# One attention's exponentials on ScalarE: the output copy between the two heads, and a wait for each head

## What is computed

```
def swa_mixer(h, w_in, q_g, k_g, sinks, memq_g, w_out, mem_k, mem_v):
    ...
    sc = jnp.where(mask[None, :, None, None], sc + bias[None, None], NEG_INF)
    ...
    p = jax.nn.softmax(jnp.concatenate([sc, sink], axis=-1), axis=-1)[..., :-1]
    o = jnp.einsum('bnhgqc,bnchd->bnqhgd', p.astype(vv.dtype), vv).reshape(b, s, SWA_Q_WIDTH)
    m = memory_attention(q_mem, memq_g, mem_k, mem_v)
    return jnp.concatenate([o, m], axis=-1) @ w_out
```

## Time and profile before

| | us |
|---|---|
| median of 3 runs | 2240.65 |
| the 3 runs | 2238.53, 2240.79, 2240.65 |
| profiled execution | 2238.2 |
| its span | 2236.4 |
| TensorE busy | 2188.2 (98%) |
| VectorE busy | 1716.2 (77%) |
| ScalarE busy | 1404.4 (63%) |
| GpSimd busy | 139.1 (6%) |

### The profile page before, as it was taken

One profiled execution on the slowest core, in us unless ns is written; L12 is line 12 of the kernel. 1 busy time (PEld: TensorE's weight loads), 2 busy tenths in 40 slices (PEclk: granted clock), 3 DMA queues, 4 the chain that ended last, 5 costly groups with the idle time before them and its releaser, 6 DMA issues.

```text
span 2236.4 us, 36111 instructions
## 1 busy us (share of the span) xinstructions
PE 2188.2 (98%) x11690; PEld 1871.0 (84%) x11690; DVE 1716.2 (77%) x2248; ACT 1404.4 (63%) x1865; POOL 139.1 (6%) x142
## 2 busy tenths in 40 slices
PE   8999998899999999999999999999999999999998
PEld 7889987778888888888888888788889888888987
DVE  7956656589999999999999999966576556657654
ACT  4264444568788888878787878744655444465543
POOL 8400005020000000000000000000010000001000
PEclk9999999999999999999999999999999999999999
DMA  6235554169999999999999999954355655435564
GB/s 223 84 121 192 183 184 151 41 219 374 350 363 378 356 350 357 374 356 361 353 374 367 367 352 359 346 170 151 122 175 190 189 185 188 149 129 168 184 197 142
DMA packets 151054, 552.00 MB, mean 247 GB/s; under 512 B 16736, under 2 KB 16864, under 8 KB 150752
## 3 DMA queue, kind: packets, MB, share of 16 engines
q1 hardware_dynamic: 150448, 548.77, 68.9%
q10 hardware_dynamic: 432, 1.02, 0.1%
HBM read 548.67 MB, written 1.05 MB: 246 GB/s over the span
## 4 chain that ended last, share of the span: by engine, by line
PE 87%; issue 7%; ACT 3%; DVE 3%; DMA 0%; POOL 0%; DVEq 0%; ACTq 0%; POOLq 0%
PE L L1997 58%; PE L L2050 10%; PE L L2509 5%; PE L L2605 3%; PE TB L2065 2%; PE L L2014 2%; PE SC L2228 2%; PE L L2168 1%; ACT SMX L759 1%; PE SC L2391 1%; PE SC L2399 1%; DVE wlo L1146 1%; PE L L2278 1%; PE SC L2135 1%; PE TB L2154 0%
## 5 line engine op out<-in xcount | busy, mean ns | idle before, releaser
L1146 DVE TENSOR_TENSOR wlo<-deep,whi 128x1024 fp32r<-128x1024 f32 x682 | 810.0, 1223 | 43.4 <-ACT whi L663 12.7
L663 ACT ACTIVATE whi<-deep 128x1024 fp32r<-128x1024 f32 x682 | 713.1, 1060 | 133.0 <-PE L L1997 130.4
L1146 DVE TENSOR_TENSOR wlo<-raw,whi 128x1024 fp32r<-128x1024 f32 x353 | 428.1, 1227 | 256.1 <-ACT whi L663 251.7
L663 ACT ACTIVATE whi<-raw 128x1024 fp32r<-128x1024 f32 x353 | 367.8, 1058 | 314.0 <-PE L L1997 151.2
L1997 PE MATMUL L<-whi,xhi 128*128 128x512 f32 (+1 forms) x1136 | 447.5, 394 | 2.8 <-DVE wlo L1146 2.4
L1997 PE MATMUL L<-whi,xlo 128*128 128x512 f32 (+1 forms) x1136 | 441.6, 389 | 0.0
L1997 PE MATMUL L<-wlo,xhi 128*128 128x512 f32 (+1 forms) x1136 | 441.3, 388 | 0.0
L1997 PEld LDWEIGHTS L<-whi,xhi 128*128 128x128 f32 x1136 | 213.7, 188 | 48.5 <-DVE wlo L1146 6.2
L1997 PEld LDWEIGHTS L<-whi,xlo 128*128 128x128 f32 x1136 | 213.6, 188 | 45.1
L1997 PEld LDWEIGHTS L<-wlo,xhi 128*128 128x128 f32 x1136 | 213.8, 188 | 42.1
L1997 PE MATMUL L<-whi,mhi 128*128 128x512 f32 x448 | 175.3, 391 | 0.0
(11 more groups left out here) (378 smaller groups left out, 3468.8 us busy)
## 6 DMA issues: line engine op xcount, KB each, us to landing
deep<-wm SPq DMA_DIRECT2D x679, 512.0 KB, 5.5
raw<-wm SPq DMA_DIRECT2D x245, 512.0 KB, 3.8
raw<-w SPq DMA_DIRECT2D x112, 512.0 KB, 4.3
mbuf<-mem SPq DMA_DIRECT2D x2, 1024.0 KB, 8.6
const<-const SPq DMA_DIRECT2D x1, 1312.0 KB, 7.5
out<-hn SPq DMA_DIRECT2D x2, 512.0 KB, 2.6
h<-x ACTq DMA_DIRECT2D x1, 512.0 KB, 4.9
h<-x SPq DMA_DIRECT2D x1, 512.0 KB, 4.7
```

The lines of the kernel that those rows point to most:

```text
L663: act(hi, slots[:, slot, :], ACT.Copy).then_inc(w.s.hi, 1)
L1146: v.tensor_tensor(lo, slots[:, slot, :], hi.bitcast(F32), ALU.subtract).then_inc(w.s.lo, 1)
```

## The change

`exps(i, heads)` now can do one head alone. For n = 1 the wait for sfree stands ahead of each head and asks for this head's scores only (x + 1 and not 2). The signal ex comes behind head 1, as before. In the loop of `attention` on ScalarE, a step that has exponentials does head 0 of pair s+2, then pair_out of s-2 (if there is one), then head 1. The calls in the second block pass no heads and do both, one behind the other, with the split wait.

```diff
-                def exps(i):
+                def exps(i, heads=(0, 1)):
                     n, causal, sinks, _ = pairs[i]
                     at = plan[i][0]
                     _, top, den, sunk = pair_stats(stat, i, n)
-                    if n == 1:
-                        e.wait_ge(w.s.sfree, w.at("s", plan[i][2] + 2 + 4))
-                    else:
+                    if n > 1:
                         e.wait_ge(w.s.mx, w.turn)
-                    for x in range(2):
+                    for x in heads:
+                        if n == 1:
+                            e.wait_ge(w.s.sfree, w.at("s", plan[i][2] + x + 1 + 4))
                         for t in range(T):
...
-                    ins.then_inc(w.s.ex, 1)
+                    if heads[-1] == 1:
+                        ins.then_inc(w.s.ex, 1)
...
-                    if s < len(steps) and j == 0 and i + ahead < len(pairs):
-                        exps(i + ahead)
+                    follows = s < len(steps) and j == 0 and i + ahead < len(pairs)
+                    if follows:
+                        exps(i + ahead, (0,))
                     if s >= 2 and steps[s - 2][2]:
                         pair_out(steps[s - 2][0])
+                    if follows:
+                        exps(i + ahead, (1,))
```

## The result

Over ten runs each the changed kernel takes 2233.28 us (median; 2232.76 to 2234.61) and the kernel before 2238.64 (2236.88 to 2240.79): 5.36 us less. The ratio is 0.9976, with a 95% interval from 0.9968 to 0.9985. The profiled execution took 2232.96, its span is 2231.2; before it was 2238.2 and 2236.4. The runs of one kernel come in groups up to 2 us apart, so a difference of a microsecond or two between medians says little by itself.

The account below looks back on a forecast made before the run. TensorE is busy 98%, so only its holes count, made by a wait ring in the second attention; 5.06 us there plus 0.2 in the second block, 5.26, off 2239.55 gives 2234.3 us, range 2230.8 to 2237.0.

Parts of the forecast that it names:

- The ring: First block's second-layer window attention: chi, clo, scores and both heads' exponentials wait for one another, 4.35 us a lap.
- its replacement: The same attention after the change: the wait loop takes 2.6 us, so TensorE's own 3.37 us a step bounds.
- pair 5: Sixth head pair of that attention, numbered from 0; its product follows 2.71 us behind, not 4.21, gaining 1.50.
- pair 2: Third head pair, counted from 0; its product with the values gains 1.75 us, as clo allows.
- pairs 3 and 4: Head pairs whose products then follow at TensorE's 3.37 us a step, not 4.34 and 4.21, gaining 0.97 + 0.84.
- Part 2: A head waits for its own scores only: first exponential at the attention's entry 0.68 us earlier.
- part 1: chi moves between the two heads' exponentials on ScalarE and can come 1.07 us earlier.
- The second rival: Thinner cover in the attention: things arrive late, gain 3.5 to 4.4 us, 2235.6, within 0.2%; chance 0.21.
- What the moved step holds up: ScalarE stands at chi for TensorE's out_turn about half a microsecond in steps 4 and 5.
- The cover at step 7: Slack of 0.5 us between ScalarE's preceding copies and TensorE's last transposes; once gone, each 0.1 costs 0.1.
- The second block: Its layers share the function: ScalarE's 1.10 us idle and TensorE's 0.37 hold shrink, 0.2 us once, bounds 0 and 0.37.
- The clock rival: Denser attention keeps TensorE's upper clock to its end: a further 2.8 us less, 2231.5; chance 0.15.

Follow-up runs that it names:

- The load experiment: A needless 128x256 ScalarE copy ahead of chi in steps 2 to 5, added to both kernels: changed 2234.46 us, before 2242.28 us.
- output first: Changed kernel, but chi is written ahead of both heads' exponentials instead of between them: 2233.56 us.
- order alone: Changed kernel, but a head's exponentials again wait for both heads' scores; chi stays between the heads: 2235.76 us, ratio 0.9984 to before.
- changed + load: Changed kernel with a needless 128x256 ScalarE copy behind head 0 and ahead of chi in steps 2 to 5: 2234.46 us.
- wait alone: Changed kernel, but chi is again written behind both heads' exponentials; each head waits for its own scores only: 2235.63 us.
- entry filled: Changed kernel with 18 unused 128x256 matmuls in TensorE's idle time ahead of the attention's head transposes: 2232.38 us, ratio 0.9976 to before.
- before + load: Kernel before with a needless 128x256 ScalarE copy behind both heads and ahead of chi in steps 2 to 5: 2242.28 us, ratio 1.0012.
- before with the tail filled: Kernel before with five unused 128x256 matmuls on TensorE in the stage's thin tail: 2237.51 us, ratio 0.9998 to before.
- tail banks: Changed kernel with the last two pairs' products and turned outputs in banks the scores no longer need: 2231.90 us.
- changed with the tail filled: Changed kernel with five unused 128x256 matmuls on TensorE in the stage's thin tail: 2231.66 us.
- all three: Changed kernel with unused matmuls at the entry and in the tail, and the last two outputs in the scores' banks: 2231.98 us.
- the entry filled by 13: Changed kernel with the last two outputs in the scores' banks and 13 unused matmuls ahead of the head transposes: 2229.16 us, ratio 0.9955 to before.

## Why the prediction was right, and where it wasn't exact

**The ring and its replacement.** Right. I had 5.06 us to pair 5 and the trace shows 5.00: the entry 0.67 (0.68), pair 2 1.74 (1.75), pairs 3 and 4 3.39 and 3.37 a step (3.37), pair 5 2.74 (2.71). The load experiment shows that the bound changed hands. That the floor is TensorE's is shown by the laps: 3.37 to 3.39 in the changed kernel, with the output first, with the order alone and under the load, each time what TensorE's own rows had given.

**Part 2** was worth the entry and a little at pair 5, 0.92 us in all, once part 1 stands; by itself 2.72. The second rival's clause, head 0's signal worth nothing, had put the rest at 4.3; the order alone has 4.08, since it also costs 0.25 at pair 5.

**What the moved step holds up.** I had ScalarE standing half a microsecond at chi in two steps; it is 0.31 twice. The cover at step 7 holds: the transposes start 0.23 behind the out_turn ahead of them (414.12 to 414.35), as they would with nothing to wait for. "Output first" takes it away and they come 0.6 later.

**The second block.** I had 0.2 us, once. The first exponential and the scores that were held 0.37:

```profile
1540.16 0.40 ACT L759 ACTIVATE hn<-hn,stat 128x128 f32<-128x128 f32 x1 [0.55 <-DVE stat L1278]
...
1545.74 0.52 PEld L2139 LDWEIGHTS SC<-qkT 64*128 64x128 f32 x8 [0.17 <-issue]
```

ScalarE idles 0.55 and not 1.10, and the hold is down to the usual 0.17. Behind L682 the trace is 0.3 shorter than before, about the 0.2 of the sum.

**The clock rival** was put as a choice: kept, or not. It is neither. In the trace after, the level fell but for 3.4 us only, and with its 1.6 us (36.05 - 34.43 from pair 5 to L682) that one execution gained more than the 5.26 of the sum; the 1.7 of offset ahead of the stage took it back, so that 2238.2 - 2232.96 = 5.24 agrees with my 5.26 partly by luck. Kernels with nearly the same tail went either way: low for 6.8 us and 36.04 (order alone), 36.05 (changed + load), 36.20 (output first); low for 3.4 us and 34.65 (wait alone), 34.62 (entry filled). The price that I gave the low stretch, 2.8, was somewhat too high: filled, the kernel before shows 2.4. The Trainium skill's "TensorE: Matmul & The Clock Gate", section "What's actually happening", has activity release the throttle; the fillings at the tail and at the entry agree with that, since matmuls whose results nobody uses kept the level at 1.00 there.

**The forecast of the time**, 2234.3 with 2230.8 to 2237.0, came from the middle of two pairs of runs, 2239.55. Ten runs put the kernel before at 2238.64, 0.9 lower, so most of my 1.0 us too much is that starting value. The difference was forecast as 5.26 and measured as 5.36; the interval of the ratio, 3.4 to 7.2 us, is much wider than this agreement. The lower end of the range doesn't follow from its own words: the clock rival off the lower pair is 2233.1 - 2.8 = 2230.3, not 2230.8. Nothing hangs on it.

**The offset outside the stage.** L734 stands at 387.2 to 387.3 or at 388.8 to 389.0 in most traces, whatever was changed behind it. The first step of this comes some 14 us into the program. Between the same two sets of TensorE transposes lie 3.37 us before and 4.97 in the changed kernel:

```profile
13.66 0.66 PE L2065 MATMUL TB<-const,hn 128*128 128x128 f32 x4 [1.12 <-DVE xlo L1193]
...
17.03 0.60 PE L2065 MATMUL TB<-const,hn 128*128 128x128 f32 x4
```

```profile
13.71 1.12 PE L2069 MATMUL TB<-const,hn 128*128 128x128 f32 x4 [1.05 <-DVE xlo L1197]
...
18.68 0.60 PE L2069 MATMUL TB<-const,hn 128*128 128x128 f32 x4
```

Its first four transposes take 1.12 us for 0.66, and the 128x256 matmuls behind them start 0.21 apart for 0.12. I take this for the lower level, at which 128x512 matmuls start 0.43 apart for 0.23 at the end of the stage in the trace of before; the clock column itself reads 1.00 there in both traces. Six of the fourteen traces have this slow start: changed, order alone, before + load, before with the tail filled, tail banks, entry filled. Of the other eight, four have L734 at 387.2 to 387.3; three (output first, changed with the tail filled, all three) lose 0.5 to 1.9 us against before between 68 and 124 us, where every trace has short low stretches, of differing place and length; the last is the one with the entry filled by 13. Behind L682 two traces stand out: before with the tail filled (1.4 us more than before) and tail banks (2.3 more than the changed kernel). Both have a low stretch near 1450 us that the other twelve haven't, and come some 1.6 us later behind it. The rows of tail banks:

```profile
1445.00:1450.00 5.00, 3.84 (x13) 2.96 (x14) 4.86 (x9) 2.69 (x6) 0.00 (x0) 0.75 0.40 129
1450.00:1455.00 5.00, 5.00 (x26) 4.11 (x25) 4.28 (x7) 1.79 (x3) 0.00 (x0) 0.91 0.51 186
```

So most of the offsets between traces come from slow stretches of TensorE at places that the change doesn't touch, and a single one is a third of what the change gains.

**What stays open:** which of these places make the groups of the runs without a trace, and why the level falls in one execution and not in another of the same code. I ran nothing on those parts.

## What to carry to other kernels

When no engine is full in a stage, write down the ring that the waits name, with its price a lap, and beside it what the busiest engine needs for a step; the gain of shortening the ring ends at that number, and two shortenings don't add up beyond it. In an in-order queue, look for the short step that another engine waits for and that stands behind long work for later: where exactly it goes matters little, as long as it is ahead. Behind the stage look at what the tail then waits for; here two free banks and matmuls on idle time were worth some 4 us, beside the change's 5.4.

## What I hadn't expected of the hardware

- Idle time of 6.4 us on TensorE at the entry costs more than itself: the 20 transposes behind it take 4.56 us to the last copy at granted clock 0.50, and 2.39 to 2.44 when the hole is filled with unused matmuls.
- The low stretch at the end of the stage costs between 0.8 and 2.6 us in traces of nearly the same code (34.43 to 36.20 from pair 5 to L682, against 33.6 filled), by its length: 3.4 us in three traces (34.43 to 34.65), 6.8 in four (36.04 to 36.20). A gain of a few microseconds read from one trace needs it taken out first.
- Elsewhere, at about 14 and 1450 us, the same code has such a stretch in one trace and not in another, for some 1.6 us each time. Two traces of kernels that differ in one stage can differ nearly as much outside it.
- A plain float32 matmul of 128x256 for filling appears as two instructions and takes 0.44 us (18 in 7.93), twice what I had counted.
